# The expert layer's last product with tokens as the stationary operand

## The reference

```python
idx = i1 * N_KEYS + i2                      # 8 heads x 16 chosen experts a token
gate = jax.nn.softmax(cs, axis=-1)
a = jnp.einsum('cd,chkd->chk', xc, peer_u[idx])
act = (jax.nn.gelu(a.astype(jnp.float32), approximate=False) * gate).astype(xc.dtype)
return jnp.einsum('chk,chkd->cd', act, peer_v[idx])
...
h = _layer_norm(ALPHA * x + tok, ln1_g, ln1_b)
return _layer_norm(ALPHA * h + _peer(h, w_query, sub_keys, peer_u, peer_v), ln2_g, ln2_b)
```

## Time and profile before

| | us |
|---|---|
| median of three timed runs | 2291.38 (2290.71 to 2291.55) |
| span of the profiled execution, first to last instruction | 2289.8 |
| median less that span: what lies around the span | 1.6 |
| phase peer_v, first to last product (1492.9 to 2270.2) | 777.3 |
| after the last product, to the end of the span | 19.6 |

### The profile page before, as it was taken

How to read it: one execution, slowest core, us unless ns; L and a number is a source line. 1 busy time by engine, 2 the same in 40 slices (tenths; PEclk the granted TensorE clock), 3 DMA queues, 4 the chain that set the end, 5 groups by cost and what they waited for, 6 DMA issues and landing times.

```text
span 2289.8 us, 48588 instructions
## 1 busy us (share of the span) xinstructions
PE 2268.3 (99%) x17591; PEld 2259.5 (99%) x17591; DVE 1491.2 (65%) x2713; ACT 884.7 (39%) x1109; POOL 1442.5 (63%) x750
## 2 busy tenths in 40 slices
PE   9999999999999999999999999999999999999997
PEld 9999999999999999999999999999999999999997
DVE  3984564354659986556556561478777778777755
ACT  5444453345544444333333333333333333333334
POOL 4876667776677777767767667755555555554025
PEclk9999999999999999999999999999999999999998
DMA  7554446554455555666666666887767777777653
GB/s 255 171 197 152 143 137 206 208 182 156 148 165 187 190 182 191 202 213 215 214 213 217 214 213 217 273 277 237 259 233 246 253 251 258 242 247 242 214 171 110
DMA packets 150512, 475.26 MB, mean 208 GB/s; under 512 B 19568, under 2 KB 42352, under 8 KB 149872
## 3 DMA queue, kind: packets, MB, share of 16 engines
q1 hardware_dynamic: 116944, 416.43, 55.5%
q10 hardware_dynamic: 24264, 40.93, 4.9%
q0 software_dynamic: 9216, 16.81, 2.4%
HBM read 433.21 MB, written 43.28 MB: 208 GB/s over the span
## 4 chain that ended last, share of the span: by engine, by line
PE 93%; DVE 5%; DMA 1%; issue 1%; ACT 1%; SPq 0%; DVEq 0%; ACTq 0%
PE ps L1562 29%; PE ps L1556 29%; PE ps L1557 29%; PE ps L1845 1%; DVE F L1092 1%; DVE F L1093 1%; PE ps L1598 1%; PE ps L1771 1%; DMA F<-gelu_scratch,F 1%; PE ps L1790 0%; DVE b_lo L1106 0%; PE ps L1605 0%; DVE R L1121 0%; PE ps L646 0%; ACT R L1046 0%
## 5 line engine op out<-in xcount | busy, mean ns | idle before, releaser
L759 POOL TENSOR_TENSOR w_lo<-raw,w_hi 128x1024 fp32r<-128x1024 f32 x452 | 1095.1, 2446 | 542.6 <-ACT w_hi L816 511.8
L816 ACT ACTIVATE w_hi<-raw 128x1024 fp32r<-128x1024 f32 x690 | 693.8, 1053 | 653.5 <-PE ps L1562 576.7
L1556 PE MATMUL ps<-a_hi,w_hi 128*128 128x288 f32 x3072 | 826.0, 295 | 0.0
L1557 PE MATMUL ps<-a_lo,w_hi 128*128 128x288 f32 x3072 | 824.3, 295 | 0.0
L1556 PE MATMUL ps<-b_hi,w_hi 128*128 128x288 f32 (+2 forms) x2432 | 629.2, 290 | 0.4 <-ACT w_hi L816 0.4
L1557 PE MATMUL ps<-b_lo,w_hi 128*128 128x288 f32 (+2 forms) x2432 | 626.7, 289 | 0.0
L1556 PEld LDWEIGHTS ps<-a_hi,w_hi 128*128 128x128 f32 x3072 | 577.1, 188 | 2.4 <-issue 2.2
L1557 PEld LDWEIGHTS ps<-a_lo,w_hi 128*128 128x128 f32 x3072 | 578.4, 188 | 0.1
L1562 PE MATMUL ps<-a_hi,w_lo 128*128 128x288 f32 x3072 | 468.5, 294 | 0.0
L791 POOL DMA_INDIRECT sample_rows<-in_peer_v,F x256 | 301.0, 1176 | 262.2 <-PE ps L1562 208.0
L1556 PEld LDWEIGHTS ps<-b_hi,w_hi 128*128 128x128 f32 x2432 | 457.9, 188 | 0.9 <-issue 0.8
(11 more groups left out here) (259 smaller groups left out, 1440.9 us busy)
## 6 DMA issues: line engine op xcount, KB each, us to landing
raw<-in_peer_u SPq DMA_DIRECT2D x256, 512.0 KB
raw<-in_peer_v SPq DMA_DIRECT2D x256, 512.0 KB
raw<-in_w_in SPq DMA_DIRECT2D x96, 512.0 KB
gelu_scratch<-F ACTq DMA_DIRECT2D x32, 576.0 KB, 6.0
gate_scratch<-g_stage ACTq DMA_DIRECT2D x36, 512.0 KB, 6.0
F<-gelu_scratch SPq DMA_DIRECT2D x32, 576.0 KB
raw<-in_w_out SPq DMA_DIRECT2D x32, 512.0 KB
raw<-in_w_query SPq DMA_DIRECT2D x32, 512.0 KB
```

The lines of the kernel that those rows point to most:

```text
L759: pool.tensor_tensor(wl[:, j, s], raw[:, j, s], wh[:, j, s].bitcast(F32), ALU.subtract).then_inc(lo_ready, 1)
L816: act.activation(wh[:, k, s], raw[:, k, s], ACT.Copy).then_inc(hi_ready, 1)
L1556: pe.matmul(out, w, mh(k), start=(n == 0), stop=False)
L1557: pe.matmul(out, w, ml(k), start=False, stop=False)
```

## The change

**The product is turned.** 128 tokens of `b_hi` or `b_lo` are now the stationary operand, and 512 output columns of rows of `peer_v` move. A "double unit" (`v_super`) is 1024 experts by 512 columns, two of the old units; there are 64. It has 48 matmuls 512 wide, 24 for the second 128 prompt tokens after 24 for the first. The 8 PSUM banks hold the sums of 256 tokens by 2048 columns through all 16 blocks: `take` is gone. To let ACT and DVE work ahead, there is a second pair of `w_hi` and `w_lo`, in place of the operands of `peer_u`; `raw` still has two slots, so one double unit.

**The sampled tokens are gathered throughout.** `ROWS` is 16, a slot is 128 by 2048, and DVE's `scalar_tensor_tensor` is 2048 wide. A slot still has its own Gelu gather. Pacing is gone: POOL issues whenever a buffer is free. DVE's list has `add_slot(k)` behind double unit `n` by the table `ADD_AT`: slots 0 and 1 at n = 0 and 1, the others some two double units apart, the last at n = 60. The gates' one-hot work is for 256 tokens, `WITH` = 8, and `gate` is 256 wide.

**Around it.** DVE does the `w_lo` of the last 8 units of `peer_u`, so POOL begins gathering earlier. h gets into the sums by 64 matmuls with an identity; the sampled tokens' h by 16 transposes; the factor ALPHA is taken out of the gates instead. The second layer norm works on token rows (`bn_stats`), by token tile; sums are normalised, turned back on PE (`turn`), scaled and stored tile by tile. The sampled tokens' chain (ACC folded from 128 to 32 partitions, statistics, scaling) is on DVE behind the loop, and PE waits for its end (`z_sample`) after the first token tile of the last double unit.

```diff
...
-          "out": (16, 1), "query": (16, 1), "peer_u": (128, 1), "peer_v": (128, 2)}
+          "out": (16, 1), "query": (16, 1), "peer_u": (128, 1), "peer_v": (64, 1)}
...
-BEFORE, WITH = 5, 9
-TOKS = T // (WITH * 8)
+BEFORE, WITH = 5, 8
+TOKS = SEQ // (WITH * 8)
 TG = TOKS * 8
...
-SPARSE = 4
-DENSE = 8 - SPARSE
-ROWS = 2 * SPARSE
...
+SUPERS = BLOCKS * COL_BANKS
+
+
+LOW_DVE = 8
+
+
 SLOTS = PH * TOPK // 4
+ROWS = 16
 RING = 2
-V_LAST = 120
+
...
+
+def added_at(k):
+
+    return k if k < RING else int(1.98 * (k - 1) + 0.6)
+
+
+ADD_AT = {added_at(k): k for k in range(SLOTS)}
 
 
 CONST = {}
...
@@ -214,9 +228,13 @@
         bh = sb("b_hi", [P, KT, TW], F32R)
         bl = sb("b_lo", [P, KT, TW], F32R)
 
-        head = 2 * 4 * T + 2 * 2 * 8 * T
...
+            with pool.Fori(FIRST_UNITS // 2, (UNIT0["peer_v"] - LOW_DVE) // 2) as i:
                 for j in range(2):
                     lower(i, j)
 
             v_rows = peer_v.rearrange("u p (r d) -> (u p r) d", d=P)
             gelus = a_dram.rearrange("a p n -> (a p n)").unsqueeze(1)
-            pool.wait_ge(rows_named, 1)
-            pool.wait_ge(outs_done, OUT0["peer_v"] + 1)
-            for n in range(2):
-                pool.wait_ge(a_stored[n], 16 * BLOCKS + 1)
-
-            def paced(k, r):
-
-
-                i, m = divmod(k, 5)
-                pool.wait_ge(outs_done, OUT0["peer_v"] + 1 + 32 * i + int(6.2 * (m + r / (ROWS + 1))))
-
-            for k in range(SLOTS):
+
+            def gather_rows(k):
                 n = k % RING
-                if k >= RING:
-                    pool.wait_ge(slot_used, k - RING + 2)
                 for r in range(ROWS):
-                    paced(k, r)
                     pool.indirect_dma_start(VROWS[:, n, r * P:r * P + P], None, v_rows,
                                             bass.IndirectOffsetOnAxis(ap=VIDX[:, k, r:r + 1], axis=0))\
-                        .then_inc(row_in[n][r], 16)
-                paced(k, ROWS)
+                        .then_inc(row_in[n], 16)
+
+            def gather_gelu(k):
                 pool.indirect_dma_start(GELU[:, k:k + 1], None, gelus,
                                         bass.IndirectOffsetOnAxis(ap=AIDX[:, k:k + 1], axis=0))\
-                    .then_inc(gelu_in[n], 16)
-            with pool.Fori((UNIT0["peer_v"] + V_LAST) // 2, UNITS // 2) as i:
-                for j in range(2):
-                    lower(i, j)
-            norm_pool(pool)
+                    .then_inc(gelu_in[k % RING], 16)
+
+            pool.wait_ge(rows_named, 1)
+            for k in range(RING):
+                gather_rows(k)
+            for m in range(2):
+                pool.wait_ge(a_stored[m], 16 * BLOCKS + 1)
+            for k in range(RING):
+                gather_gelu(k)
+            for k in range(RING, SLOTS):
+                pool.wait_ge(slot_used, k - RING + 2)
+                gather_rows(k)
+                gather_gelu(k)
 
...
-
-            act.wait_ge(ln_pe, 3 + 2)
-            act.activation(MEAN, LNP[0], ACT.Copy).then_inc(ln_mean, 1)
-            act.wait_ge(ln_var, 2)
-            act.activation(S3[:, 2], S3[:, 1], ACT.Sqrt).then_inc(ln_sqrt, 1)
-            for e in range(AFFINE):
-                act.wait_ge(n_aff, KT + e + 1)
-                act.activation(R[:, e, :], R[:, e, :], ACT.Identity, scale=V("g2")[:, e:e + 1],
-                               bias=V("b2")[:, e:e + 1]).then_inc(y_normed, 1)
+            act.activation(tiny[:, 1:2], tiny[:, 0:1], ACT.Sqrt)
+
+            def hi_v(u):
+
+                n, k = u // 2, u % 2
+                if n == 1:
...
-            def lower(u, j):
+            def lower(unit, high, low, j):
 
                 for h in range(2):
-                    ve.wait_ge(hi_ready, 2 * (UNIT0["peer_v"] + u) + h + 1)
+                    ve.wait_ge(hi_ready, 2 * unit + h + 1)
                     s = slice(h * HU, h * HU + HU)
-                    ve.tensor_tensor(wl[:, j, s], raw[:, j, s], wh[:, j, s].bitcast(F32), ALU.subtract)\
+                    ve.tensor_tensor(low[:, j, s], raw[:, j, s], high[:, j, s].bitcast(F32), ALU.subtract)\
                         .then_inc(lo_dve, 1)
...
-            def add_slot(i, n):
-
-
-                k, b = 10 * i + n, n % RING
-                for r in range(ROWS):
-                    ve.wait_ge(row_in[b][r], 16 * (5 * i + n // RING + 1))
-                ve.wait_ge(gelu_in[b], 16 * (5 * i + n // RING + 1))
-                link(ve.tensor_tensor(GATED[:, b:b + 1], GELU[:, bass.ds(k, 1)], EG[:, bass.ds(k, 1)], ALU.mult))
+            def lower_super(n):
+
+                for j in range(2):
+                    lower(UNIT0["peer_v"] + 2 * n + j, WH[n % 2], WL[n % 2], j)
+
+            def add_slot(k):
+
+                b = k % RING
+                ve.wait_ge(row_in[b], 16 * ROWS * (k // RING + 1))
+                ve.wait_ge(gelu_in[b], 16 * (k // RING + 1))
+                link(ve.tensor_tensor(GATED[:, b:b + 1], GELU[:, k:k + 1], EG[:, k:k + 1], ALU.mult))
                 ve.wait_ge(slot_used, k + 1)
                 ve.scalar_tensor_tensor(out=ACC, in0=VROWS[:, b, :], scalar=GATED[:, b:b + 1], in1=ACC,
                                         op0=ALU.mult, op1=ALU.add).then_inc(slot_used, 1)
 
...
+            ve.tensor_copy(ident_r[:, :], ident).then_inc(ident_set, 1)
...
-            norm_first(ve, own, link, 1, take_last, 1.0)
-            norm_last(ve, link)
+            for j in range(LOW_DVE):
+                lower(UNIT0["peer_v"] - LOW_DVE + j, wh, wl, j % 2)
+                if j >= 4:
+                    ve.wait_ge(blk_in[0], 64)
+                    for e in range(2 * j - 8, 2 * j - 6):
+                        gate(0, e)
+            lower_super(0)
+
+
+            for n in range(SUPERS - 1):
+                b, q = divmod(n, COL_BANKS)
+                lower_super(n + 1)
+                if b + 1 < BLOCKS:
+                    if q == 0:
+                        ve.wait_ge(blk_in[(b + 1) % 2], 64 * ((b + 1) // 2 + 1))
+                        ve.wait_ge(outs_done, OUT0["peer_v"] + n + 1)
+                    for e in (2 * q, 2 * q + 1):
+                        gate((b + 1) % 2, e)
+                if n in ADD_AT:
+                    add_slot(ADD_AT[n])
+
+                if b == BLOCKS - 1 and q > 0:
+                    ve.wait_ge(outs_done, OUT0["peer_v"] + n + 1)
+                    for t in range(TOK_TILES):
+                        row_stats(ve, P, 1 + t, q - 1, y_bank(t, q - 1))
+                if b == BLOCKS - 1 and q == 1:
+                    ve.tensor_copy(Z[:, 0, 0, :], y_bank(0, 0)).then_inc(bank0_free, 1)
+
...
+            other = VROWS[:, 0, :]
+            ve.wait_ge(slot_used, SLOTS + 1)
+            link(ve.tensor_copy(other[0:64], ACC[64:128]))
+            link(ve.tensor_tensor(ACC[0:64], ACC[0:64], other[0:64], ALU.add))
+            link(ve.tensor_copy(other[0:NS], ACC[NS:2 * NS]))
+            link(ve.tensor_tensor(ACC[0:NS], ACC[0:NS], other[0:NS], ALU.add))
+            for c in range(COL_BANKS):
+                last = row_stats(ve, NS, 0, c, ACC[0:NS, 512 * c:512 * c + 512])
+            link(last)
+            row_variance(ve, link, NS, 0)
+            ve.wait_ge(outs_done, OUT0["peer_v"] + SUPERS)
+            for t in range(TOK_TILES):
+                row_stats(ve, P, 1 + t, 2, y_bank(t, 2))
+            mean, r = row_rstd(ve, link, NS, 0)
+            ve.tensor_scalar(other[0:NS], ACC[0:NS], mean, r, ALU.subtract, ALU.mult).then_inc(z_sample, 1)
+
...
+                for q in range(4):
+                    e = 4 * c + q
+                    last = ve.tensor_scalar(YT[:, e, P * t:P * t + P], y_bank(t, c)[:, P * q:P * q + P],
+                                            V("g2")[:, e:e + 1], V("b2")[:, e:e + 1], ALU.mult, ALU.add)
...
+            for t in range(TOK_TILES):
+                ve.wait_ge(y_summed, t + 1)
+                link(row_stats(ve, P, 1 + t, 3, y_bank(t, 3)))
+                row_variance(ve, link, P, 1 + t)
...
+                    y_dve_bank(t, c)
+
 
 
         @block.tensor
...
+            def tokens(a, s, e, t):
+
...
+            def rows(w, n, e):
+
...
+            def y_sum(n, t):
+
...
+            def v_high(n, s, e, t):
+
+                pe.matmul(y_sum(n, t), tokens(bh, s, e, t), rows(WH, n, e), start=False, stop=False)
+                pe.matmul(y_sum(n, t), tokens(bl, s, e, t), rows(WH, n, e), start=False, stop=False)
+
+            def v_low(n, s, e, t, stop=False):
+
+                return pe.matmul(y_sum(n, t), tokens(bh, s, e, t), rows(WL, n, e), start=False, stop=stop)
+
...
+            def v_super(i, k, ends=False):
+
+                n, s = 8 * i + k, k // COL_BANKS
+                if k % COL_BANKS == 0:
+                    pe.wait_ge(act_ready, 16 * i + 8 * s + 8)
+                high_in(16 * i + 2 * k + 1)
+                for t in range(TOK_TILES):
+                    for e in range(8):
+                        v_high(k, s, e, t)
+                    if t == 0:
```

(51 more changed lines are left out.)

352 lines of the change are left out of this document (144 added, 208 removed).

## The result

The changed kernel takes 2365.76 us (median of 4 runs, 2364.26 to 2371.86), the kernel before 2291.47 us: a ratio of 1.0329, 95% interval 1.0315 to 1.0344. It is slower by 74 us. The forecast was 2337 us, 46 us slower than before, with a range of 2255 to 2375. The profiled execution has a span of 2363.0 us.

A forecast was written before the change was run, and what follows sets the result against it. POOL's gathers, held up by DVE, were to set peer_v's pace after the change: 2289.8 - 777.3 + 816 + 3.5 + 3.4 = 2335.4 us of span, plus 1.6 to the timed median, so 2337 us; range 2255 to 2375.

The forecast's parts named there:

- The signs that the prediction named: Profile after: DVE waits for slots some 30 times, POOL hardly idle, issues 1.15 to 1.3 us, matmul starts 221 to 238 ns apart.
- rows 4 and 5: Profile before, POOL issues beside DVE subtractions: undisturbed 0.95 us, otherwise ending 0.82 us after the subtraction; read as an early access held.
- the Trainium skill's inference on descriptors: POOL's gathers: descriptor generation needs only the write side, so a plain tensor_tensor on DVE would not hold it up.
- The rivals in which POOL is free or nearly so: peer_v: POOL not held up, 2213 us, chance 0.14; or held little, 2284 us, faster 0.16, within 0.2% 0.04.
- transfers bind on top: Rival in peer_v: gather bursts meet the loads of raw, each double unit loses 0.5 us, some 2370 us; chance 0.08.
- start of the phase, later by: Small terms before peer_v: fewer one-hot steps -3.8 us, 16 transposes +1.8, 64 identity matmuls +5.5; together +3.5 us.
- 30 slots: POOL's slots in peer_v after the first two: 17 issues each, 25.9 us a slot, 777 us in all.
- the stall: Delay of a POOL issue by DVE instructions in peer_v: 0.27 us each, on top of 1.25 us.
- PE's rate: 512-wide matmuls in peer_v: 225 ns each, a double unit 10.8 us, 64 of them 691 us (679 to 731).
- The first rival: peer_v: POOL is not held up and PE stays in charge, phase 691 us, kernel 2213 us; chance 0.14.
- PE's idle time: peer_v: PE idles some 4 us per slot, behind DVE's w_lo or gating.
- The tail: Kernel's end: PE waits 8 us for the sampled tokens' chain, 11 us behind the last sum; 23 together, +3.4 us.

The follow-up runs named there:

- e1: Changed kernel with peer_v laid out so a slot's rows come by 8 gathers of 256 values instead of 16 of 128: 2238.87 us, ratio 0.9766.
- e3: Changed kernel with each gather bringing 64 values instead of 128, same number of gathers, other halves cleared to zero: 2394.07 us, ratio 1.0443.
- e2: Changed kernel without the gathers and DVE's additions of slots: 2229.90 us, ratio 0.9727; last product 720.0 us.
- e7: Changed kernel with DVE copying raw into w_lo instead of subtracting, and all gathers spread by waits on DVE's progress: 2278.27 us, ratio 0.9943.
- e4: Changed kernel with DVE copying raw into w_lo instead of subtracting (low parts wrong), gathers not spread: 2400.39 us, ratio 1.0471.

## Why the prediction was right, step by step

**Side and mechanism.** POOL, held up by DVE, sets the phase's pace through DVE's wait in order: shown by the chain and the waits, by e1 and e3 together (count, not bytes), by e2 (without it 136 us go) and by e7 (less hold, shorter slots). The signs that the prediction named came too: 29 waits of DVE for a slot, one wait of POOL for a buffer, issues of 1.28 us on average, starts 231 ns apart. One reading went too far: rows 4 and 5 show that an issue is held up, not by which of its accesses. The gathers read their indices from SBUF, so that they don't contradict the Trainium skill's inference on descriptors ("SBUF — State Buffer", Who interferes with whom); its rule on GpSimd instructions that read SBUF would do, and no run here tells the two apart. The rivals in which POOL is free or nearly so are out; "transfers bind on top" is out too, though its price, 2370 us, lies nearest to the time.

**The sum.** The mechanism was right and the size too small: 46 us slower were forecast and 74 came, 9 us inside the upper end of the range. 2363.0 of span against 2335.4, 27.6 us, in the prediction's own terms:

| term | predicted | measured |
|---|---|---|
| start of the phase, later by | 3.5 | 3.6 |
| until POOL may begin slot 2 (1496.5 to 1509.5) | 11 | 13.0 |
| 30 slots (1509.5 to 2307.8) | 777 | 798.3 |
| from there to the last sum (28, and 12 of the tail) | 40 | 43.6 |
| behind the last sum (2351.35 to 2363.0) | 11 | 11.65 |

The mis-sized term is the stall, worth 21 of the 27.6 us. The measured mean distance of issues behind the first addition is 1.566 us, that is 1.25 + 0.32, where I took 0.27; a slot took 26.6 us, not 25.9. Rows 4 to 7 had led me to 0.30, and I had pulled it toward the mean of before, 0.23. But in before the issues were spaced by PE's progress, and here they come one behind the other into DVE's four subtractions, so that the old mean was no guide. What holds fits the prediction's reading: 537 of 544 issues end within 60 ns of that reading, which is 0.95 us after their start, or, where DVE was in an instruction with two inputs in SBUF as the issue began, 0.82 us after that instruction's end, if this is later. Six of the other seven began within 0.03 us of the start of DVE's instruction and took 0.95 us.

**PE's rate.** I took 225 ns for a 512-wide matmul, with 221 and 238 as bounds. The median distance of starts over the 3072 of the phase is 231 ns; three of them (start, us, line, op):

```profile
1719.95 0.40 PE L1882 MATMUL ps<-w_hi_more,b_hi 128*128 128x512 f32 x1
1720.18 0.40 PE L1883 MATMUL ps<-w_hi_more,b_lo 128*128 128x512 f32 x1
1720.42 0.39 PE L1882 MATMUL ps<-w_hi_more,b_hi 128*128 128x512 f32 x1
```

3072 x 0.231 = 710 us, 19 above my 691; with two waits in the last double unit, 8.0 us together, it gives e2's 720.0, nearly. The first rival's 2213 us (its terms add up to 2212) would have been 2230. It decided nothing here, since PE was not in charge. The Trainium skill's 216 ns ("TensorE: Matmul & The Clock Gate", Back-to-back issue gap) falls further short. The same section calls it the gap of an isolated matmul and gives some 131 ns at 512 for a stream of weight loads and matmuls; this stream of fp32r took 231.

**PE's idle time.** Foreseen as 4 us in each slot. It came as 20 gaps of 5.4 us on average, 108 us, and 164 matmuls at the lower clock, 35 us more; 710 + 108 + 35 = 853 is the phase to within 2 us. The end of the chain shows such a stretch, behind the wait for the sampled tokens (start, us, what):

```profile
2342.61 0.43 PE ps L1883
...
2345.59 0.43 PE ps L1882
...
2346.36 0.23 PE ps L1882
2346.59 0.23 PE ps L1883
```

0.43 us is 512 columns at 1.2 GHz (the granted clock from 2342 to 2346 us is 0.50 of full speed); from 2346.4 us on PE is back at 2.4 GHz. As long as POOL set the pace, PE would have waited in any case, so there the lower clock should have cost nothing (no run tests it); here, where PE was awaited, it did cost some 2 us, and the prediction had left it out.

**The tail.** PE waited 5.4 us for z_sample (8 predicted); turning, normalising and storing fit to 1 us.

**Not foreseen.** That the other engines can stand still beside a run of gathers. The changed kernel itself doesn't suffer from it: between 1440 and 1500 us PE had no gap. Only e1, e3 and e4 showed it, so it has no part in the 74 us.

## What to carry to other kernels

Count the instructions of the engine that issues the software gathers, and price each at its issue distance plus what DVE holds it up; where a gather can bring a longer contiguous piece, lay the data out for that, since here the bytes were free and the issues cost 1.25 to 1.57 us each. When a change takes work off the bounding engine, check whether the next one's list still fits the new, shorter period: here 21.4 us were asked for and 26.6 needed. Look at what the other engines do beside a burst of software gathers, even where POOL has nothing else to do; where they stand still, spread it by waiting on another engine's progress. In the executions recorded here that was worth 9, 33 and 122 us, though the cause is open.

## What the runs showed of the hardware

- fp32r matmuls with a weight load each are 119 ns apart at 256 columns, 131.7 at 288 and 231 at 512.
